# The expert stages' result store, cut from one transfer into four on ScalarE's queue

## The reference, cut to what matters

```
for e in range(N_EXPERTS):
    act = jax.nn.silu(hf @ w_gate[e]) * (hf @ w_up[e])
    out = out + combine[:, e:e + 1] * (act @ w_down[e])
```

## Time and the profile before

| | |
|---|---|
| median of 3 runs | 3503.95 us (3492.57 to 3511.65) |
| the profiled execution | 3507.12 us |
| its span, first to last instruction | 3505.5 us |
| mean granted TensorE clock | 0.831 of full speed |
| blocks in the three expert stages | 44, 52, 52 |
| busy: TensorE matmuls, VectorE, ScalarE, GpSimd | 71%, 30%, 15%, 11% of the span |

### The profile page before, as it was taken

The page is one execution under the profiler, slowest core; times in us unless marked ns, Lnnn a source line. Parts: engine busy times, 40 slices in busy tenths (PEclk is TensorE's granted clock), DMA queues, the critical chain, the costliest instruction groups (busy, mean ns, idle before and its releaser), DMA issues. The chain is left out here.

```text
span 3505.5 us, 74506 instructions
## 1 busy us (share of the span) xinstructions
PE 2491.8 (71%) x31542; PEld 1793.8 (51%) x31543; DVE 1037.5 (30%) x2767; ACT 520.8 (15%) x1257; POOL 370.8 (11%) x527
## 2 busy tenths in 40 slices
PE   8987957685998746754353897999998954556642
PEld 4465545464446445533242345989986443444431
DVE  0235321124008421210014303556555420111104
ACT  1133100011105000000001102323321010000000
POOL 0000110002000110000002001112113110000002
PEclk9998968797999868977686898888887877778876
DMA  5202159886110168999996100000002169998794
GB/s 203 86 28 109 61 197 325 327 318 231 54 72 25 45 234 311 337 355 386 368 364 238 44 24 1 1 0 0 0 0 82 73 231 378 359 345 327 273 387 179
DMA packets 101173, 646.48 MB, mean 184 GB/s; under 512 B 28690, under 2 KB 50450, under 8 KB 67300
## 3 DMA queue, kind: packets, MB, share of 16 engines
q1 hardware_dynamic: 41440, 567.30, 42.3%
q0 software_dynamic: 32896, 55.23, 4.9%
q10 hardware_dynamic: 26756, 22.82, 2.0%
HBM read 599.98 MB, written 45.09 MB: 184 GB/s over the span
## 5 line engine op out<-in xcount | busy, mean ns | idle before, releaser
L1165 PE MATMUL ps<-ring,arena 128*32 128x128 f32 x13440 | 414.4, 283 | 133.2 <-DVE arena L1208 89.8
L1174 PE MATMUL ps<-ring,arena 128*32 128x256 f32 x3360 | 266.4, 451 | 330.1 <-DVE arena L1223 325.3
L1165 PEld LDWEIGHTS ps<-ring,arena 128*32 128x32 f32 x13440 | 394.7, 115 | 171.7 <-issue 153.7
L1220 DVE TENSOR_TENSOR arena<-arena,ps 128x64 f32<-128x64 f32 x296 | 63.4, 214 | 977.0 <-ACT arena L1198 977.0
L1174 PEld LDWEIGHTS ps<-ring,arena 128*32 128x32 f32 x3360 | 118.8, 126 | 433.3 <-issue 369.9
L1198 ACT ACTIVATE arena<-ps 128x64 f32<-128x64 f32 x296 | 60.4, 223 | 1457.3 <-issue 831.6
L1174 PE MATMUL ps<-xt_mem,arena 128*32 128x256 f32 x1376 | 115.6, 478 | 191.9 <-DVE arena L1223 191.6
L1140 POOL DMA_DIRECT2D arena<-xybuf x148 | 100.5, 679 | 1400.6 <-DVE arena L1208 1354.7
L1165 PE MATMUL ps<-arena 128*32 128x128 f32 x5504 | 166.5, 279 | 18.6 <-issue 17.7
L1165 PEld LDWEIGHTS ps<-arena 128*32 128x32 f32 x5504 | 159.2, 113 | 34.1 <-issue 30.3
L1174 PEld LDWEIGHTS ps<-xt_mem,arena 128*32 128x32 f32 x1376 | 51.8, 132 | 236.9 <-issue 216.5
(11 more groups left out here) (385 smaller groups left out, 3838.5 us busy)
## 6 DMA issues: line engine op xcount, KB each, us to landing
ring<-in_experts SPq DMA_DIRECT2D x165, 2048.0 KB, 20.6
arena<-in_experts SPq DMA_DIRECT2D x50, 2048.0 KB, 22.2
xt_mem<-in_experts SPq DMA_DIRECT2D x25, 2048.0 KB, 24.2
ring<-in_mixer_chunks SPq DMA_DIRECT2D x24, 2048.0 KB, 12.4
xybuf<-arena ACTq DMA_DIRECT2D x160, 128.0 KB
arena<-xybuf POOLq DMA_DIRECT2D x160, 128.0 KB, 11.9
xybuf<-arena SPq DMA_DIRECT2D x1, 9216.0 KB, 25.6
rows<-in_ln_g POOLq DMA_DIRECT2D x6, 512.0 KB, 5.1
```

Source lines behind the costliest of these rows:

```text
L1165: ins = pe.matmul(ps[at, 2 + half, 0:P], xg[:, k, :], w_gu[half][:, k, q, :], start=(k == 0), stop=(k == NK - 1))
L1174: ins = pe.matmul(ps[at, 4, 0:W], hT[:, f, :], w_d[:, f, q * W:(q + 1) * W], start=(f == 0), stop=(f == NT - 1))
L1220: dve.tensor_tensor(hidden[:, half, :], silu_g[:, half, :], ps[:, 2 + half, HALF:P], ALU.mult)\
```

## The change

The store is issued as four transfers, one for each quarter: 32 partitions of `y_sb` to 32 rows of `xybuf`, 256 columns each. Two are issued ahead of the first silu and two between the silus. Each counts `s_stored[b]` up by 16, so the waits on it now count in 64s. The spare stores and the last store are cut in the same way. The rows and bytes written are the same (block g - 1 begins at row g x 32 of `xybuf`).

```
-            def spare_rows(b):
-                return xybuf[(SPARE_BLOCK + b) * BLK:(SPARE_BLOCK + b + 1) * BLK, :].rearrange("r (q n) -> q r n", q=4)
-
...
                 @block.scalar
                 def _(act):
+                    def store_quarters(start, b, two):
+                        for q in two:
+                            act.dma_start(xybuf[bass.ds(start, BLK), q * W:(q + 1) * W], y_sb[quarters[q], b, :])\
+                               .then_inc(s_stored[b], 16)
+
                     for b in range(AHEAD - 1):
-                        act.dma_start(spare_rows(b), y_sb[:, b, :]).then_inc(s_stored[b], 16)
+                        store_quarters((SPARE_BLOCK + b) * BLK, b, range(4))
...
                             act.wait_ge(s_y, g + 1)
-                            act.dma_start(rows_at(g - 1), y_sb[:, freed, :]).then_inc(s_stored[freed], 16)
                             for half in range(2):
+                                store_quarters(g * BLK, freed, (2 * half, 2 * half + 1))
                                 act.wait_ge(s_gu[half], g + 1)
                                 act.activation(silu_g[:, half, :], ps[:, 2 + half, 0:HALF], ACT.Silu).then_inc(s_silu[half], 1)
                     act.wait_ge(s_y, AHEAD * fours + 1)
-                    act.dma_start(rows_at(AHEAD * fours - 1), y_sb[:, AHEAD - 1, :]).then_inc(s_stored[AHEAD - 1], 16)
+                    store_quarters(AHEAD * fours * BLK, AHEAD - 1, range(4))
                     for b in range(AHEAD):
-                        act.wait_ge(s_stored[b], fours * 16 + 16)
+                        act.wait_ge(s_stored[b], fours * 64 + 64)
...
-                            dve.wait_ge(s_stored[b], p * 16 + 16)
+                            dve.wait_ge(s_stored[b], p * 64 + 64)
```

## The result

The changed kernel takes **3371.19 us** (median of 4, 3361.7 to 3372.7) against 3503.97 us (3492.57 to 3511.65) for the kernel before: ratio 0.9618, 95% interval 0.9586 to 0.965. It gained 133 us where 153 were forecast; the range held it.

What follows compares the result with a forecast made beforehand. The weight stream bounds the expert stages, ScalarE's long store issues stalling 53 blocks. Stalls -50, -39, -52, evening out -32 and give-back +20 sum to -153, giving 3350 us; range 3265 to 3460, the forecast's own 3265 to 3415.

Steps and rivals of the forecast that it cites:

- The mechanism: Block stores: 32-row transfers use 16 engines, 192 packets a store, 12 per engine in place of 33, so no long issue.
- The issues: ScalarE's three more store issues per block, at 0.45 to 0.66 us each, hidden behind TensorE's work: taken as nothing.
- The stalls: Expert stages: blocks run 5.45 us apart once weights arrive, so the three stages end 50, 39 and 52 us earlier.
- the rival of the packet turns: Quick blocks: 12 packet turns per block beside weights exceed 5.45 us, VectorE's copy waits for stores; 3459 us, chance 0.10.
- My bound for a wrong forecast: VectorE's copy at L1230: the prediction is wrong if its waits for stores grow past 150 us.
- The evening out: Weight loads: store packets spread over all engines save 0.15 us on each of 216 loads, -32 us.
- The give-back: Experts of three to five blocks let the weight stream run dry; seven restarts cost +20 us, between 0 and 40.
- "Issue" waits gone: Sign on ScalarE: silu's waits that end in "issue", 831.6 us in 53 before, disappear.
- TensorE waiting for weights: Sign in the expert stages: TensorE waits for the weight transfers instead of silu waiting behind long issues.
- DMA share near 0.95: Sign in the expert stages: DMA engines' busy share rises to near 0.95 from 0.89, 0.93 and 0.91.
- Ends near 785, 1770 and 3300: Sign: the three expert stages end near these times in us, where they ended at 837, 1867 and 3454.
- Loads longer than 5.9 us: Sign of a wrong prediction: weight loads take longer than 5.9 us because all engines now carry small packets.

Runs made afterwards that it cites:

- e2b: Changed kernel with each 32-row transfer's destination taken as 4 groups of every fourth row, so four engines each: 3517.28 us, ratio 1.005.
- e3: Changed kernel with two store transfers of 64 partitions per block, one ahead of each silu, two engines each: 3675.98 us (one execution).
- e1: Changed kernel with one store transfer per block, written as 128 consecutive pieces of 1 KB over 16 engines: 3347.69 us, ratio 0.9549.
- e8: Kernel before, its single 4x32x256 store issued behind both silus of the block instead of ahead: 3522.61 us, ratio 1.0056.
- e4: Changed kernel with all four store transfers issued ahead of the first silu: 3370.83 us, ratio 0.9613.
- e6: Changed kernel with only the first of a block's four store transfers issued, the rest left out: 3318.48 us, ratio 0.9488.
- e2: Changed kernel with destination rows written as 4 groups of 8 consecutive rows; the split was not kept, so the changed kernel ran again: 3369.77 us, ratio 0.9614.
- e5: Changed kernel with GpSimd's load of each block's input also cut into four transfers of 32 rows: 3275.1 us, ratio 0.9362.
- e7: Changed kernel with GpSimd loading only the first column quarter of each block's input in the loop: 3215.28 us, ratio 0.9193.
- e9: Kernel before, store in one transfer as it was, with GpSimd's input load cut into four transfers of 32 rows: 3450.86 us, ratio 0.9853.

## Why the prediction was right, and where its sizes were off

**The mechanism held.** 32 rows took 16 engines, 192 packets a store with 16 marks for each transfer, and no issue was long. e2b took away the spread alone, and the gain and the short issues went with it; e3 halved the engines, and the time went up by 171 us. e1 gave back the single instruction but kept the spread, and was the faster. e8 moved the old store behind the silus and won nothing.

**The issues, forecast 0: right.** An issue is 322 ns, under the 450 to 660 assumed. Quick blocks stay 5.45 us apart, and e4, which doubles what stands before the first silu, has the same time.

**The stalls, forecast -50, -39 and -52.** Stages two and three were 42 and 53 us shorter. Stage one was only 24 shorter, or 31 with its earlier start: it ended at 805, not 787. This is the term that failed by size. The weights were there in time, the last at 757.4 where I had 762. But TensorE turned to the last expert only at 778.4, and the end came 48 us after that landing, not 25: the wrong term is the stage's end. VectorE waited 99.0 us for stores in 21 waits and the blocks had fallen behind. That is the rival of the packet turns, which I had taken for all or nothing: with 12 packets per engine and a weight packet between each two (from 600 to 740 us q1 moved 3229 packets and q10 3227), a store four blocks back (22 us at 5.45 a block) isn't always done: a transfer lands up to 32.6 us after its issue. It cost some 20 us, not 109, by the two runs that lighten the store and leave the rest, e1 (9 packets) and e6 (a quarter of them): both take 287 us, and from the last landing to the end 23 (e2, the same as the changed kernel, had 305, so this is 18 to 23). e5 and e7 keep the 12 packets: their stage one is shorter by their earlier weights alone, and from the last landing to the end it is 48 and 49 us as in the changed kernel. The argument against the rival, that it corrects itself when weights pause, was right: behind 757.4 the copies wait for TensorE again and the blocks are some 5.45 us apart. My bound for a wrong forecast, 150 us of waits at L1230's copy, was passed, with 174.6. Most of that cost nothing, since e1 has none of these waits and is only 24 us faster.

**The evening out, forecast -32: measured 0.** From one landing of SP's 2 MB loads to the next, where the next was already issued, the mean was 6.29, 5.86 and 5.86 us in the three stages before, and 6.42, 5.91 and 5.91 after: no gain, if anything a little lost. I had named the reason as a bound, that GpSimd's loads may set the pace, and took a value between. They do set most of it: e6 with a quarter of the stores keeps 5.84 in stage two, while e7 with a quarter of the loads has 5.33, 5.22 and 5.18. By 39, 90 and 87 loads that would be 168 us; e7 is 156 us under the changed kernel. A load does wait for its last mark, as the estimate had it: in the kernel before, the 12 loads that landed from 1590 to 1660 did so 0.5 to 0.7 us after the last of their 16 marks ended, and 2.5 to 4.3 us lay between the first end and the last, where it is 1.3 for a load alone (2706 to 2722). My estimate read the packets of the stores and left out that each input load still goes in its old layout, 4x32x256, which costs 96 us by e5.

**The give-back, forecast +20: measured 0.** I counted seven restarts of the stream. Summed over all times inside the stages with no weight load issued and not yet landed, from the first load to the last landing, the kernel before had 18.9, 25.8 and 41.0 us, together 86; the changed one has 2.6, 0 and 0. The pauses that I expected for experts of three to five blocks don't happen.

**Not foreseen: the start of the stages, -14.** After the scatter GpSimd waits until its rows have landed and then issues the first input loads of stage one (L1135 before, L1132 after):

```profile
489.26 2.85 POOL L1135 DMA_DIRECT2D arena<-xybuf  x4 [9.62 <-issue]
...
482.92 2.84 POOL L1132 DMA_DIRECT2D arena<-xybuf  x4 [6.17 <-issue]
```

From the issue of the last scatter to that of the first load it took 10.6, 9.9 and 10.0 us in the three stages before and 7.1, 6.5 and 6.9 after, 10 us together. The spare stores are on the queue just then, and the other runs show that their layout sets this time: with the store on two engines (e3) it is 12.2 to 13.8 us, on four (e2b, e8, e9) 8.7 to 10.4, on sixteen with 12 packets each 6.5 to 7.3, with 9 (e1) 5.9 to 6.3. Another 3 us of the 14 had arisen before the scatter of stage one (469.7 and 466.8), where the two kernels do the same: that is chance, since the kernels of this study reach it anywhere from 460.3 to 469.8. The forecast took nothing for the spare stores, and priced only the three more behind the last block, not the nine more ahead of the first.

The terms as measured: -120 for the stages (24, 42, 53), -14 for their starts, 0 for the pace and 0 for restarts: -134, against -135 between the two profiled executions (3507.12 and 3372.45). The forecast of -153 had two wrong terms, -32 and +20, that in part cancelled, stage one 26 too good, and lacked the 14. That these left only 20 us is luck; that the range held is not, since the two that made the forecast too good, 32 and 26, are together less than the 65 us on its upper side. (Its lower bound should have read 3276: 3350 less 54 and 20.)

**The signs.** "Issue" waits gone: in part, since a third of the us is left under that name though no long issue is. TensorE waiting for weights: yes. DMA share near 0.95: it is 0.99 to 1.01. Ends near 785, 1770 and 3300: they are 805, 1787 and 3320, each 17 to 20 late, so all of it arose in stage one. Loads longer than 5.9 us as a sign of failure: 5.91 in stages two and three and 6.42 in stage one, where they had been 5.86 and 6.29. I had set this bound at what the loads already took, so it told nothing.

## What to carry to other kernels

Look at how many DMA engines a transfer uses, by its packets when it moves alone (here 132, the four over its 128 rows being its marks): with a size of 4 outermost on the DRAM side one store used four engines, and beside the weight stream its queue advanced by one small packet per weight packet on each of them, one per 0.63 us (24.3 for 24.7). Reorder the access so that a larger size stands outermost (here 128 or 32 for the 4), if you can in one transfer (e1), otherwise in several (the changed kernel, 133), and do it for the loads beside the stream as well (e5, 96 us more). The long issues here ended with some 104 packets in the queue for each engine used, which I read as a full queue: moving the issue moved the wait (e8, 3522.61 against 3502.87 us).

## What was unexpected of the hardware

- Two transfers on two engines each made the kernel 5% slower than one on four (3675.98, a single execution, against 3505.39 us).
- Long issues ended with 418 packets in the queue by the median on four engines and 212 on two (e3), 104 to 106 per engine; but with e2b's four transfers a store on four engines they ended with 321, 80 per engine. So the limit isn't one number of packets alone; what else counts is open.
- The issue's own time varies with the layout: by the median 322 ns for 32 rows over 16 engines, 339 for 128 pieces over 16 (e1), 559 for 128 over four, 634 for 32 rows over four (e2b), 530 for 64 over two (e3).
- A dimension split that describes rows in a row changed nothing (e2: 36356 packets on q10, as in the changed kernel); one that takes every fourth row did (e2b: 144 a store instead of 192).
- Input loads of 128 KB, 160 in all beside 567 MB of weights, cost a lot: leaving out three quarters of each is worth 156 us (e7), and their layout alone 96 (e5): 380 GB/s with them whole, 407 with them cut, and a DMA share of 1.01 in both. A whole load moves as 32 packets of 4 KB and 112 small ones, with three or more of the 32 under way in 9% of the time in which any was (1400 to 1700 us of the changed kernel); one cut in four as 64 of 2 KB and 64 marks. Whether the size of the packets or the engines that they use holds up the weights was not settled.
